# A root mean square taken out of the operand: the first block's input projections run undivided, and VectorE divides each one as it leaves PSUM

## The reference, cut to what matters

```python
def _rms_norm(x, weight):
    x = x * jax.lax.rsqrt(jnp.mean(x * x, axis=-1, keepdims=True) + EPS)
    return x * weight
...
h = ...                                 # 16 meta tokens and 256 tokens, 1024 wide
proj = _rms_norm(h, attn_norm) @ w_in   # 17 blocks of 128 columns
```

## Time and profile before

| | us |
|---|---|
| time, median of 3 runs | 1490.41 (1485.09 to 1490.55) |
| the profiled execution's own time | 1496.24 |
| its span, first to last instruction | 1494.5 |

### The profile page before, as it was taken

How to read it: one execution, slowest core, us unless ns; L and a number is a source line. 1 busy time by engine, 2 the same in 40 slices (tenths; PEclk the granted TensorE clock), 3 DMA queues, 4 the chain that set the end, 5 groups by cost and what they waited for, 6 DMA issues and landing times.

```text
span 1494.5 us, 31410 instructions
## 1 busy us (share of the span) xinstructions
PE 1434.7 (96%) x11038; PEld 1352.7 (91%) x11038; DVE 1016.9 (68%) x2084; ACT 684.3 (46%) x1035; POOL 557.1 (37%) x252
## 2 busy tenths in 40 slices
PE   6999998999899999999999999999999988999997
PEld 5787668999899999999999999999989957799997
DVE  4424544889888888877676666666555745599997
ACT  4432644445355555543333333444454345555553
POOL 3313227778800000024444444444423325254441
PEclk9989989999999999999999999999999978999999
DMA  7410125666655555557877777555553504256552
GB/s 278 142 58 29 43 85 176 191 192 192 185 194 175 175 175 175 176 185 228 238 230 232 232 230 229 177 190 182 183 171 120 175 20 144 76 186 188 184 174 80
DMA packets 89994, 250.16 MB, mean 167 GB/s; under 512 B 10048, under 2 KB 35920, under 8 KB 89296
## 3 DMA queue, kind: packets, MB, share of 16 engines
q1 hardware_dynamic: 86112, 238.20, 51.2%
q10 hardware_dynamic: 3824, 11.17, 2.1%
HBM read 234.09 MB, written 15.24 MB: 167 GB/s over the span
## 4 chain that ended last, share of the span: by engine, by line
PE 80%; DVE 6%; POOL 6%; issue 5%; ACT 1%; DMA 0%; ACTq 0%; POOLq 0%; DVEq 0%
PE ps L1651 37%; PE ps L2027 28%; POOL w_lo L494 6%; PE ps L2010 4%; PE ps L1915 2%; PE ps L1869 2%; PE ps L1666 1%; PE ps L1889 1%; PE ps L1840 1%; DVE big L1071 1%; DVE w_lo L1049 1%; PE ps L1730 1%; PE ps L1761 0%; ACT w_hi L595 0%; DVE big L1063 0%
## 5 line engine op out<-in xcount | busy, mean ns | idle before, releaser
L494 POOL TENSOR_TENSOR w_lo<-raw,w_hi 128x1024 fp32r<-128x1024 f32 x193 | 504.5, 2617 | 804.7 <-ACT w_hi L595 804.7
L1651 PE MATMUL ps<-x_op,w_hi 128*128 128x256 f32 (+1 forms) x3968 | 748.9, 290 | 22.0 <-DVE x_op L1067 8.8
L1651 PEld LDWEIGHTS ps<-x_op,w_hi 128*128 128x128 f32 x3968 | 627.2, 194 | 35.3 <-issue 20.5
L1651 PE MATMUL ps<-x_op,w_lo 128*128 128x256 f32 (+1 forms) x1984 | 567.2, 286 | 0.0
L595 ACT ACTIVATE w_hi<-raw 128x1024 fp32r<-128x1024 f32 x400 | 420.5, 1055 | 266.5 <-PE ps L2027 214.4
L2027 PE MATMUL ps<-h_op,w_hi 128*128 128x256 f32 x2400 | 426.7, 279 | 2.4 <-DVE h_op L1601 2.4
L1651 PEld LDWEIGHTS ps<-x_op,w_lo 128*128 128x128 f32 x1984 | 385.2, 194 | 0.0
L2027 PEld LDWEIGHTS ps<-h_op,w_hi 128*128 128x128 f32 x2400 | 367.8, 188 | 3.1 <-issue 1.8
L1049 DVE TENSOR_TENSOR w_lo<-raw,w_hi 128x1024 fp32r<-128x1024 f32 x207 | 265.4, 1282 | 114.2 <-ACT w_hi L595 114.0
L2027 PE MATMUL ps<-h_op,w_lo 128*128 128x256 f32 x1200 | 337.2, 281 | 0.0
L2027 PEld LDWEIGHTS ps<-h_op,w_lo 128*128 128x128 f32 x1200 | 225.2, 188 | 0.0
(11 more groups left out here) (267 smaller groups left out, 1057.6 us busy)
## 6 DMA issues: line engine op xcount, KB each, us to landing
raw<-blocks SPq DMA_DIRECT2D x404, 512.0 KB, 3.7
early_store<-kv_mem SPq DMA_DIRECT2D x96, 128.0 KB, 1.7
work<-early_store SPq DMA_DIRECT2D x96, 128.0 KB, 4.0
big<-consts ACTq DMA_DIRECT2D x2, 1336.0 KB, 6.6
big<-h_t ACTq DMA_DIRECT2D x4, 272.0 KB, 3.8
big<-bias_lines ACTq DMA_DIRECT2D x8, 136.0 KB, 2.6
bias_lines<-route_t ACTq DMA_DIRECT2D x4, 264.0 KB, 2.9
res<-mem_t SPq DMA_DIRECT2D x1, 1024.0 KB, 9.3
```

The lines of the kernel that those rows point to most:

```text
L494: pool.tensor_tensor(w_lo[:, s, :], raw[:, s, :], w_hi[:, s, :].bitcast(F32), ALU.subtract).then_inc(sem("lo_pool"), 1)
L1651: mm = pe.matmul(ps[:, m_bank, 0:T], w, x, start=(k == 0 and j == 0), stop=(k == last and j == 2))
```

## The change

The input's high part is now the input times its norm weight, rounded (`gained_in` on ScalarE), and VectorE takes all 8 low parts in one instruction each (`lower_in`). Neither waits for the root. The inverse root is kept in `in_rb` (in the memory of `kv_mem`), and `scale_in(j)` on VectorE replaces `evacuate_in(j)`: it multiplies projection `j` in PSUM by `in_rb` while it moves it out, in one instruction for 8 of the projections and in two for the 9 of which the squares are needed (j = 4 to 12; ScalarE then squares in SBUF, `follow_in`). VectorE squares half of the input. The weights' low part of block 0 goes from GpSimd to VectorE and that of block 1 from VectorE to GpSimd. On TensorE `relative_line(0)` stands behind projection 1 instead of 0, line 1 behind projection 2, line 2 behind 3 and line 3 behind 4. ScalarE issues the load of the constants after it has rounded blocks 0 to 2, and no longer ahead of the rounding of block 0. The multiplications of the memory stand behind block 5's low part.

```diff
     if B_QUERY <= n < B_V + 2:
         return "pool" if n < B_BESIDE else "dve"
+    if n < 2:
+        return ("dve", "pool")[n]
     return "pool" if n % 2 == 0 else "dve"
...
             pool.memset(two_in, 0.0).then_inc(sem("windows_zero"), 1)
-            los(B_IN, B_IN + 1)
-            norm_lo(R_ATTN, NK)
-            los(B_IN + 1, B_IN + 9)
+            los(B_IN, B_IN + 9)
...
+            gained_in(range(4))
+            his(1)
+            gained_in(range(4, KT))
             root(R_ATTN, NK)
-            his(2)
+            his(3)
             act.dma_start(cst, dram["consts"][:, N_CONSTS_KEPT:]).then_inc(sem("cst_loaded"), 16)
...
-            norm_hi(R_ATTN, NK, 0)
...
+            def follow_in(j):
+
                 his(B_IN + j + 3)
...
+                if 4 <= j < 13:
+                    act.wait_ge(sem("bank_free"), M_IN + j + 1)
+                    squared(rope_sq if j == 4 else dq_sq[:, j - 5, :] if j < 9 else dk_sq[:, j - 9, :])
...
-            norm(R_ATTN, h_t, "attn", NK)
...
+            lower_in(range(4))
+            los(B_IN + 1)
+            lower_in(range(4, KT))
+            dve.wait_ge(sem("rms_root"), R_ATTN + 1)
+            step(dve.reciprocal(in_rb, rt[:, 0:NK]))
+
+            def scale_in(j):
+
+                dve.wait_ge(sem("block_used"), B_IN + j + 1)
+                b = ps[:, (M_IN + j) % 2]
...
+                    dve.tensor_tensor(raw_out, b[:, at], in_rb[:, at], ALU.mult)
+                    ins = dve.scalar_tensor_tensor(out=dst, in0=b[:, at], scalar=pcol(gain), in1=in_rb[:, at],
+                                                   op0=ALU.mult, op1=ALU.mult)
+                else:
+                    ins = dve.tensor_tensor(proj[:, j if j < 4 else j - 8, :], b[:, 0:NK], in_rb, ALU.mult)
+                ins.then_inc(sem("bank_free"), 1)
...
             project_in(0)
+            project_in(1)
             pe.wait_ge(sem("rel_ready"), 1)
             pe.wait_ge(sem("cst_loaded"), 16)
             relative_line(0)
-            project_in(1)
-            relative_line(1)
             norm(R_MEM, NQ, bank=3)
             project_in(2)
-            relative_line(2)
+            relative_line(1)
             latent_sum(0)
             project_in(3)
+            relative_line(2)
+            project_in(4)
             relative_line(3)
-            project_in(4)
             pe.wait_ge(sem("rms_root"), R_MEM + 1)
             latent_sum(1)
```

More of the change, by code:

```diff
@@ L639, in _, with gained_in @@
             act.wait_ge(sem("par_loaded"), 16)
-            for c in range(4):
+            for c in range(2):
                 act.wait_ge(sem(f"h_loaded{c}"), 16)
-                squares(flat2(h_t)[:, 2 * c * NK:2 * (c + 1) * NK], 2 * c, NK, 2)
+                act.activation(sq[:, 2 * c * NK:2 * (c + 1) * NK], flat2(h_t)[:, 2 * c * NK:2 * (c + 1) * NK], ACT.Square
+                               ).then_inc(sem("rms_squares"), 2 if c == 0 else KT - 2)
+            def gained_in(tiles):
+                for k in tiles:
+                    act.wait_ge(sem(f"h_loaded{k // 2}"), 16)
+                    act.activation(x_k(0, k, NK), h_t[:, k, :], ACT.Copy, scale=pcol("attn", k)).then_inc(sem("rms_hi"), 1)
+            gained_in(range(4))
+            his(1)
+            gained_in(range(4, KT))
             root(R_ATTN, NK)
-            his(2)
+            his(3)
             act.dma_start(cst, dram["consts"][:, N_CONSTS_KEPT:]).then_inc(sem("cst_loaded"), 16)
@@ L1109, in _, with mem_norm @@
             ins.then_inc(sem("heads_set"), 1)
+            scale_in(1)
             los(B_IN + 4)
+            scale_in(2)
             dve.wait_ge(sem("rms_root"), R_MEM + 1)
             step(dve.reciprocal(mem_rb, mem_rt))
[L1114 to L1117, removed]
+            def mem_norm():
+                for k in range(KT):
+                    ins = dve.scalar_tensor_tensor(out=mem_t[:, k, :], in0=mem_t[:, k, :], scalar=pcol("mem", k), in1=mem_rb,
+                                                   op0=ALU.mult, op1=ALU.mult)
+                ins.then_inc(sem("rms_xf"), KT)
             def latent_norm(w):
@@ L1130, in _ @@
             latent_norm(0)
+            scale_in(3)
             los(B_IN + 6)
+            mem_norm()
+            scale_in(4)
             latent_norm(1)
             los(B_IN + 8)
+            scale_in(5)
             dve.wait_ge(sem("bank_free"), M_IN + 5)
@@ L1138, in _ @@
             dve.tensor_tensor(rope_kc, rope_k, con("cos", QK, cst)[NOPE:QK, :], ALU.mult).then_inc(sem("rope_kc_ready"), 1)
+            scale_in(6)
             los(B_IN + 10)
@@ L1145, in _ @@
                               ).then_inc(sem("qk_turned_read"), 1)
-            los(B_IN + 12)
+            scale_in(7)
+            los(B_IN + 11)
             dve.wait_ge(sem("qk_turned_read"), 1)
             dve.tensor_tensor(q_mla, q_mla, rope_a[:, :, 0:NQ], ALU.add).then_inc(sem("q_ready"), 1)
+            scale_in(8)
+            los(B_IN + 12)
+            scale_in(9)
+            los(B_IN + 13)
+            scale_in(10)
             dve.wait_ge(sem("qk_turned"), 2)
@@ L1696, in _ @@
             pe.wait_ge(sem("ones_set"), 1)
-            norm(R_ATTN, NK)
+            for k in range(KT):
+                if k >= KT // 2:
+                    pe.wait_ge(sem("late_squares"), k - KT // 2 + 1)
+                norm_sum(R_ATTN, k, NK)
             def project_in(j):
@@ L1809, in _ @@
             pe.wait_ge(sem("k_root"), 1)
-            pe.wait_ge(sem("bank_free"), M_IN + 13)
+            pe.wait_ge(sem("in_squares"), 9)
             for h in range(DH):
```

92 lines of the change are left out of this document (50 added, 42 removed).

## The result

The changed kernel takes 1500.72 us (median of 6 runs, 1496.12 to 1505.93); the kernel before took 1489.03 on the same chip (6 runs, 1485.09 to 1490.55). The ratio is 1.0078, 95% interval 1.0055 to 1.01: slower, by some 12 us, and outside the range of the prediction. The profiled execution, 1496.12, is the fastest of the six, while that of the kernel before, 1496.24, is 7 us above its kernel's median. So the two profiles are equally long, and only their parts can be compared.

What follows compares the result with a forecast made beforehand. TensorE, busy for 96% of the span, was taken as the bound. 6.1 us gained, less 2.9, 1.9 and 2.2, made it 0.9 us slower, a median of 1491.3 us; range 1484 to 1497.5.

Steps and rivals of the forecast that it cites:

- The start: Up to line 0's end: projection 0 no longer waits for the root and starts at 12.05; 6.1 us gained.
- the constants: Their load, issued at about 14.4, takes 6.5 us, so line 0 on TensorE waits 1.7 us.
- The wait for the last line: TensorE's query product waits 2.9 us, because GpSimd's low part holds VectorE's eight memory multiplications.
- its clock step: Half clock in the query product behind the 2.9 us wait: costs 1.5 to 3 us, taken as 2.2.
- rival A: GpSimd doesn't hold VectorE at the memory multiplications: wait 0.7, no half clock, 3.5 us gained, 1486.9 us; chance 0.27.
- The values: TensorE's `values(2)` waits 1.9 us for the first value copy, which stands behind a square on ScalarE.

Runs made afterwards that it cites:

- the loop turned: VectorE's expert value loop jumps back behind the multiplication by G of an even chunk, in the kernel before (1490.3 us) and in the changed kernel (1487.5 us).

## Why the prediction was wrong

**The step that failed** is "Behind 133.48 the change alters nothing, so what it gains or loses up to there should arrive whole at the end". The operations there are the same, but the change lays VectorE's program out anew and makes a jump back 0.13 to 0.16 us longer, which cost 8 to 10 us in a loop of 290. With the loop turned in both kernels, that effect is out: 1487.5 against 1490.3, 2.9 less, where I had forecast 0.9 more; the intervals of the two overlap. For the change itself the forecast of no measurable difference held; for the kernel as it stands none of my cases had the mechanism. Why the gap at the later jumps is 0.09 us in one program and 0.22 or 0.32 in another stays open. The Trainium skill (page "Advanced Engine Details and Errata", section "Control Flow Timing") gives about 51 ns for a branch and 108 for a compare-and-branch; if a jump back takes one of each, that is 0.16 us, an estimate from that page. Without a jump, the multiplication's record overlaps the one ahead of it by 0.08, so the jump costs 0.17 us in the kernel before, which is near it, and 0.30 in the changed kernel, which is not. The skill (page "Runtime: NRT & Kernel Launch", section "Instruction fetch mechanics") also says that a jump out of the two blocks of instructions on hand must wait for a fetch. The traces speak against a fetch at each jump: in 24 rounds of the loop (655 to 940 us) the queues marked instruction moved 3 packets in all, in the kernel before, in the changed kernel and in the one with 8 memsets alike.

**The start** came as worked out, but for the constants. The timeline of the changed kernel (with ScalarE's issues) has projection 0 at 12.11 (forecast 12.05) and the wait for GpSimd's low part 0.89 (0.9). The constants were issued at 12.31, not 14.4, since ScalarE's issue stands ahead of its roundings in the records; they took 8.4 instead of 6.5, and line 0 waited 1.21 (1.7):

```profile
12.11 0.52 PE L1708 MATMUL ps<-x_op,w_hi 128*128 128x272 f32 x2 [0.86 <-DVE w_lo L1051]
12.31 0.35 ACTq L658 DMA_DIRECT2D big<-consts  x1
16.29 0.52 PE L1708 MATMUL ps<-x_op,w_hi 128*128 128x272 f32 x2 [0.89 <-POOL w_lo L497]
...
20.79 1.12 PE L1766 MATMUL ps<-big,work 32*128 32x264 f32 x4 [1.21 <-DMA big<-consts]
21.85 5.41 PE L1723 MATMUL ps<-big,ones 128*128 128x256 f32 x16
```

Behind this wait the granted clock read 0.68 of full speed from 21.92 to 27.3, so the memory's norm took 5.4 us where it had taken 3.65: some 1.7 that I had not charged there. That the wait for the constants came out near the forecast is luck: the issue was 2.1 us earlier and the transfer 1.9 longer, and the two cancel.

**The wait for the last line** was neither 2.9 nor 0.7 but either, by chance. The same kernel, first profile, and again:

```profile
37.10 3.25 DVE L1156 SCALAR_TENSOR_TENSOR res<-res,par,big 128x256 f32<-128x256 f32 x8
...
38.91 3.66 POOL L497 TENSOR_TENSOR w_lo<-raw,w_hi 128x1024 fp32r<-128x1024 f32 x1 [7.74 <-ACT w_hi L596]
...
42.54 4.76 PE L1821 MATMUL ps<-big 128*96 128x256 f32 x21 [0.61 <-ACT route_t L668]
```

```profile
37.08 5.36 DVE L1156 SCALAR_TENSOR_TENSOR res<-res,par,big 128x256 f32<-128x256 f32 x8
38.88 2.48 POOL L497 TENSOR_TENSOR w_lo<-raw,w_hi 128x1024 fp32r<-128x1024 f32 x1 [7.75 <-ACT w_hi L596]
...
44.62 9.92 PE L1821 MATMUL ps<-big 128*96 128x256 f32 x32 [2.71 <-ACT route_t L668]
```

GpSimd arrives between two of eight VectorE instructions that follow each other without a gap, at the same time to 0.03 us. Once it stays out until all are done (3.66), once it gets in and holds the sixth of them (5.36). The second is my forecast and its clock step: wait 2.71 (2.9), and the product took 9.92 us at a granted clock of 0.72 instead of 6.93, 3.0 lost (2.2). The first is rival A; there the whole product took 7.14 at full clock (the row shown is its first part). Of eleven profiles with this part of the change two took 5.36 and nine 3.25, so A was the likelier, not mine. With the line's copy moved ahead, the 5.36 leaves a wait of 0.9 only:

```profile
PE ps L1838 <- ACT route_t L668: 0.9, 1, 0.9
```

**The values** were right to the decimal, a wait of 1.9, in both profiles of the changed kernel; what stands behind it in the forecast is four estimates, so the decimal is luck:

```profile
70.52 1.89 PE L1782 MATMUL ps<-big 128*16 128x512 f32 x4 [1.90 <-ACT work L698]
```

**The stage as a whole** ended at 130.9 and 138.8 in two executions of the changed kernel and between 130.5 and 135.9 in nine profiles whose stage is that of before (mean 134.1; 132.5 for six profiles of the changed stage as it is). The projections ended at 128.9 and 136.8, where I had forecast 134.4. The gain of the change is smaller than what one execution differs from the next. A part of that difference is a term that my sum lacks: in the first profile the change is 1.6 us ahead when the value heads are done, near 80 us, and 4.6 at the stage's end, since TensorE got more clock from there on (0.86 against 0.78 in the kernel before, over the last 36 and 39 us).

## What to carry to other kernels

When an edit upstream slows a loop that it does not touch, look for two engines that start within 0.1 us of each other on a shared path: the loop may have had a lucky phase, and any edit can end it. Put the jump back of a loop where its engine waits anyhow. And compare variants only after such a race is out, or each verdict is on the race: memsets of 0.4 us at 198 us cost 16 us here.

## What the runs showed of the hardware that was new to me

- VectorE's two-input instructions and GpSimd's subtraction exclude each other whole: 0.42 becomes 2.60 us behind GpSimd, 2.41 becomes 2.62 behind VectorE. The Trainium skill (page "SBUF — State Buffer", section "Who interferes with whom") says that whoever is issued first holds the other, and all the fences of the loop agree. But the start of a record is not the moment of entry: at 38.91 GpSimd's record had begun when five of the eight instructions had, and the other three went ahead of it as well. The row at 118.01 in the earlier trace rows reads the same way: its record began 1.05 us ahead of VectorE's, which went first.
- VectorE's rounding from SBUF, one input, is held as well: 1.08 us (673.47) and 2.27 (668.23) instead of 0.30.
- The jump back of VectorE's loop cost 0.17, 0.30 or 0.40 us by program (the gap at the later jumps and the 0.08 of overlap), and the first one up to 0.7.
